# One inference step of a hybrid mLSTM/conv decoder layer: decode rows by VectorE's block transposes and DMA, and state updates as four 32-row tiles

## Chip, cores and metric

One core of one Trainium2 chip runs the whole layer. The metric is the device time in microseconds (us) of one launch.

## The reference, cut to what matters

A layer is: half a SwiGLU feed-forward (FFN), a mixer, half a second FFN, with a root-mean-square norm before and after each. The input has a prompt of 256 tokens and 8 decode sequences of 4 tokens each (32 decode tokens), 288 tokens in all, with 2048 features. The mixer projects to q, k, v, an output gate (4 heads of 256), to two halves of a gated causal convolution of width 31 over 1024 channels, and to an input and a forget gate for each head. For each head and sequence it computes

```
C_t = f_t C_{t-1} + i_t k_t v_t^T          n_t = f_t n_{t-1} + i_t k_t
h_t = o_t * (q_t C_t) / max(|n_t . q_t|, exp(-m_t))
```

in a chunkwise form with the running maximum m as stabiliser. A decode sequence starts from its own state C (256x256 for each head and sequence), n and m; its new state is `C_new = g_state * C + sum over its 4 tokens of g_key * k v^T`. All is float32. The outputs are the tokens, the new C, n, m and the convolution's history.

## The kernel before, in words

Features lie on the 128 partitions, tokens in the free dimension. All large products are weight tiles of 128x128 (stationary) against 288 tokens (moving). To keep float32's precision with one-pass matmuls, weights and activations are split into a high and a low part, and each product is three matmuls: high by high, high by low, low by high (`multiply`, L477 to L484).

**The stream of pieces.** The weights are one stream of 656 pieces of 128x1024 (8 tiles, 24 matmuls). SyncE's queue loads piece g into slot g mod 4 of `raw` as soon as the low part of piece g-4 is made (L428 to L435). ScalarE makes the high part `whi` (`split_hi`, L891, three pieces ahead of the matmuls), VectorE or GpSimd the low part `wlo` (L1312, L1859). TensorE works through the pieces. The first FFN has 264 pieces, the mixer's projections begin at piece 266 (`HEAD_P`) and have 94 more (`MIX`), then come the output projection and the second FFN.

**The mixer.** Its projection tiles are ordered by hand. `KEYS_AT` (8, 30, 54, 78) is the piece at which head h's k, v and q tiles begin; `CONV_AT` and `GATE_O_AT` are the same for convolution and output gate. Each engine's program runs over the same piece number p, and for each head h does in step k = p - KEYS_AT[h] what the hand-written order says (`head_part` in L1123, L1652, L2008; `gate_part` in L1193, L1757, L2032). TensorE puts a head's small matmuls between the tiles of the stream (`between`, L777): at (k, j) they stand after tile j of piece k.

For head h the steps that the change touches are:

- k = 8: ScalarE copies the 32 decode columns of k and v four times side by side (`kv4`, L1155); VectorE transposes the prompt's values in blocks of 32x32 (L1668). k = 10: ScalarE's queue stores those to DRAM (`store_squares`, L1115), and k = 12 loads them back token by token (`vtok`, L1178).
- (9, 5): TensorE transposes `kv4` in four matmuls (`to_token_major`, L670). k = 10: ScalarE copies the result three times (`vs`, `v4`, `k4`, L1166 to L1168). k = 11: VectorE makes the low parts in place, in other quarters of the partitions (L1681, L1685). So `k4` and `v4` hold the decode rows as 4 groups of 32 partitions, high and low parts such that one matmul over 128 partitions sums the three products.
- k = 12, 13: ScalarE masks `v4` for each of the 8 sequences (`vm`, L1187).
- k = 12: VectorE scales the decode queries (`qw`) and multiplies by the old normaliser `n0` (L1694 to L1703); k = 13 the masked scores; k = 14 the decode part of the convolution, with the taps read from SBUF (`conv_decode`, L1617); k = 15 the denominators.
- TensorE: scores (13, ..), `query_memory` (`QUERY_AT`: 32 matmul instructions on four tiles of 32 columns side by side, L707), `attend` (`ATTEND_AT`, L732 to L736, into banks 5 and 6).
- `update_memory` (L739): for each of the 8 sequences two matmuls of 128 rows and 256 columns into bank 4 or 7, at k = 16 to 18 plus `LATE` (2, 0, 0, 3); VectorE adds each to C (L1741).
- The gate: VectorE multiplies the heads in banks 5 and 6 (L1765), ScalarE makes the high part `mh` (L1206), VectorE the low part `ml` (L1769, counts `mix_ready`). For head 3 these are at GATE_O_AT[3] + 6 and + 7, pieces 96 and 97.
- k = 19: ScalarE's queue stores the weighted keys (L1115 again).

Of the kernel before, what the change touches and what calls it, by code (L numbers as in the profile page):

```python
# [23 lines left out]
F32 = mybir.dt.float32  # L24
# [82 lines left out]
Q_GROUP = 4  # L107

# [67 lines left out]
def hybrid_layer_kernel(nc, stream, x_in, vecs, gate_w, gate_vec, c_in, n_in, conv_in,  # L176
                        y_out, cp_out, np_out, cs_out, ns_out, m_out, conv_out):
    with ExitStack() as ctx:
# [38 lines left out]
        turned_v = nc.dram_tensor("turned_v", [SEQ // NS, NS, DC, H, P // NS, NS], F32, kind="Internal").ap()  # L217
        turned_k = nc.dram_tensor("turned_k", [SEQ // NS, NS, DC, H, P // NS, NS], F32, kind="Internal").ap()
# [10 lines left out]
        mh = place("mh", [P, D_MLSTM // P, TOK], F32R)  # L229
        ml = place("ml", [P, D_MLSTM // P, TOK], F32R)  # L230
# [11 lines left out]
        vtok = place("vtok", [P, 2, DH])  # L242
        k4 = place("k4", [P, DH], F32R)
        v4 = place("v4", [P, DH], F32R)
# [12 lines left out]
        vm = place("vm", [P, NB, DH], F32R)  # L257
        late_kv = place("late_kv", [P, 2, 2, H * DH], F32, xl_at)
# [7 lines left out]
        mask4 = place("mask4", [P, 4, NB], F32, prod_at)  # L266
# [8 lines left out]
        mask = place("mask", [P, NB])  # L275
# [9 lines left out]
        def squares(h):  # L285
            flat = prod[:, :, :, :].rearrange("p t b k -> p (t b k)") if h < H - 1 else bc[:, 0, :]
            return flat[:, 0:DC * SEQ].rearrange("p (c s) -> p c s", c=DC)

        key_squares = qkvo[:, 2, :, :].rearrange("p c t -> p (c t)")[:, 0:DC * SEQ].rearrange("p (c s) -> p c s", c=DC)

        ysum = rpost
        own = bass.AP(ident, 0, [[P, P], [Q_GROUP * NT, NB // Q_GROUP], [NS + NT, Q_GROUP], [1, NT]])
        qct = sq[:, :, :].rearrange("p a t -> p (a t)")[:, 0:DH]
        kv4 = cpr[:, :, :].rearrange("p c e -> p (c e)").rearrange("p (a c m) -> p a c m", a=2, c=DC)
        psum = ctx.enter_context(nc.psum_tensor("bank", [P, 8, 512], F32))
        bank = [psum[:, i, :] for i in range(8)]

# [36 lines left out]
        tr_done, dec_hi, dec_lo, vm_ready, tr_evicted = (sem("tr_done"), sem("dec_hi"), sem("dec_lo"),  # L334
                                                         sem("vm_ready"), sem("tr_evicted"))
        kv4_ready = sem("kv4_ready")
# [17 lines left out]
        nn_ready = sem("nn_ready")  # L354
        cap_ready, cap_added = sem("cap_ready"), sem("cap_added")
        turn_ready, sums_ready = sem("turn_ready"), sem("sums_ready")
# [26 lines left out]
        def four(ap):  # L383

            return ap.unsqueeze(2).broadcast_to([P, DC, P // NS, NS])
# [19 lines left out]
        def _(sp):  # L405
# [22 lines left out]
            with sp.Fori(2, PIECES // SLOTS) as m:  # L428
                for s in range(SLOTS):

                    sp.wait_ge(lo_ready[s], m * 1)
                    sp.dma_start(raw[:, s, :], stream[m * SLOTS + s]).then_inc(landed[s], 16)
# [32 lines left out]
        def _(pe):  # L465
# [204 lines left out]
            def to_token_major(h):  # L670

                pe.wait_ge(kv4_ready, h + 1)
                pe.wait_ge(col_ready, 1)
# [6 lines left out]
                mm.then_inc(tr_done, 1)  # L680

            def scores(h):

                pe.wait_ge(tile_evicted, tile_of(h, "q1") + 1)
                pe.wait_ge(dec_lo, h + 1)
# [5 lines left out]
                for c in range(DC):  # L691
                    mm = pe.matmul(bank[7][:, SEQ + P:SEQ + P + NS], kv4[:, 0, c, :], q[:, c, SEQ:TOK],
                                   start=(c == 0), stop=(c == DC - 1))
                mm.then_inc(sc_done, 1)

            def query_memory(h):
# [7 lines left out]
                for r in range(NB // Q_GROUP):  # L704
                    for c in range(DC):
                        for j in range(Q_GROUP):
                            mm = pe.matmul(bank[4][NS * j:NS * (j + 1), 0:DH], qw[:, c, r, :],  # L707
                                           C[:, r * Q_GROUP + j, c, :], start=(r + c == 0),
# [13 lines left out]
            def attend(h):  # L722

                pe.wait_ge(v_landed, 32 * (h + 1))
                pe.wait_ge(sums_ready, h + 1)
                pe.wait_ge(qc_evicted, h + 1)
                if h:
                    pe.wait_ge(mix_ready, 2 * h)
                for e in range(DC):
                    out = bank[5 + e]  # L730
                    cols = slice(e * P, (e + 1) * P)
                    pe.matmul(out[:, 0:SEQ], vtok[:, 0, cols], st[:, 0:SEQ], start=True, stop=False,  # L732
                              skip_group_check=True)
                    pe.matmul(out[:, P:SEQ], vtok[:, 1, cols], st[:, SEQ:SEQ + P], start=False, stop=True,
# [4 lines left out]
            def update_memory(h, b):  # L739

                if b < 2:
                    pe.wait_ge(den_ready if b == 0 else qc_evicted, h + 1)
                else:
                    pe.wait_ge(cu_evicted, NB * h + b - 1)
                pe.wait_ge(vm_ready, NB * h + b + 1)
                out = bank[4 if b % 2 else 7]
                for c in range(DC):
                    mm = pe.matmul(out[:, c * DH:(c + 1) * DH], k4[:, c * P:(c + 1) * P], vm[:, b, :],  # L748
                                   start=True, stop=True)
                mm.then_inc(cu_done, 1)  # L750

            def prompt_memory(h):
# [7 lines left out]
                for c in range(DC):  # L760
                    for t in range(2):
                        v = late_kv[:, 0, t, :].rearrange("p (c h e) -> p c h e", c=DC, h=H)[:, :, h, :]
# [14 lines left out]
            def between(p, j):  # L777


                for h in range(H):  # L780
# [3 lines left out]
                    if (k, j) == (9, 5):  # L784
                        to_token_major(h)
# [9 lines left out]
                    if b is not None:  # L795
                        update_memory(h, b)
# [1375 lines left out]
```

## Time and profile before

| what | value |
|---|---|
| median of 3 runs | 2153.84 us (2153.32 to 2154.47) |
| the profiled execution | 2154.55 us, of which the span of the instructions is 2152.8 |
| TensorE matmuls busy | 2145.0 us, 100% of the span, 16248 instructions |
| VectorE / ScalarE / GpSimd busy | 982.1 (46%) / 891.3 (41%) / 959.4 (45%) |
| DMA | 377.69 MB, 175 GB/s, about half of the 16 engines' time |
| granted TensorE clock | full, in all 40 slices |

A matmul's duration in the profile is from its start to the end of its results and overlaps with the next ones; what it costs in a stream is the distance from its start to the next start. The sum of idle times in front of a group is shown behind it with what released the engine.

### The profile page before, as it was taken

What the parts mean: (1) busy time and instruction counts of PE and PEld (TensorE: products, weight loads), DVE (VectorE), ACT (ScalarE), POOL (GpSimd) and SP (SyncE); (2) the same over time, 40 slices, a digit from 0 to 9 for tenths busy, and PEclk for the clock granted to TensorE, in tenths of its full rate; (3) what the DMA queues carried; (4) which work ended last, traced back from release to release, by engine and by line L of the source; (5) the groups of instructions that cost most, each with busy time, mean ns of one, the idle gap of its engine ahead of it and who ended that gap; (6) DMA issues with size and microseconds to landing.
All of it is one profiled execution on the core that took longest, in us unless ns stands there. A gap on an engine that the chain in (4) does not pass through costs nothing.

```text
span 2152.8 us, 41799 instructions
## 1 busy us (share of the span) xinstructions
PE 2145.0 (100%) x16248; PEld 2134.2 (99%) x16248; DVE 982.1 (46%) x1422; ACT 891.3 (41%) x1151; POOL 959.4 (45%) x563
## 2 busy tenths in 40 slices
PE   9999999999999999999999999999999999999998
PEld 9999999999999999999999999999999999999998
DVE  6533432223434324987769738543432223333323
ACT  6434333334343335644345446434333333333443
POOL 1444443434444445476756332444443334444444
PEclk9999999999999999999999999999999999999999
DMA  7454455545554554566766554555455545454653
GB/s 250 165 169 162 164 168 169 163 161 172 164 167 158 174 165 149 204 195 237 242 198 223 200 164 145 170 165 167 157 172 169 166 157 171 161 173 157 210 165 130
DMA packets 121860, 377.69 MB, mean 175 GB/s; under 512 B 28552, under 2 KB 33804, under 8 KB 120496
## 3 DMA queue, kind: packets, MB, share of 16 engines
q1 hardware_dynamic: 97632, 349.00, 49.2%
q10 hardware_dynamic: 24016, 27.42, 4.0%
q8 instruction: 62, 1.02, 0.2%
q14 instruction: 22, 0.18, 0.0%
q0 software_dynamic: 128, 0.07, 0.0%
HBM read 361.26 MB, written 15.18 MB: 175 GB/s over the span
## 4 chain that ended last, share of the span: by engine, by line
PE 99%; DVE 0%; DMA 0%; SPq 0%; ACT 0%; issue 0%
PE bank L484 30%; PE bank L482 30%; PE bank L483 30%; PE bank L537 1%; PE bank L544 1%; PE bank L548 1%; PE bank L826 1%; PE bank L828 1%; PE bank L827 1%; PE bank L748 0%; PE bank L707 0%; DMA raw<-stream 0%; PE bank L689 0%; DVE x_res L1416 0%; DVE bank L1415 0%; PE bank L732 0%
## 5 line engine op out<-in xcount | busy, mean ns | idle before, releaser
L1864 POOL TENSOR_TENSOR wlo<-raw,whi 128x1024 fp32r<-128x1024 f32 x331 | 794.5, 2402 | 851.8 <-ACT whi L898 771.9
L482 PE MATMUL bank<-xh,whi 128*128 128x288 f32 x3344 | 992.2, 297 | 0.0
L483 PE MATMUL bank<-xl,whi 128*128 128x288 f32 x3344 | 988.3, 296 | 0.0
L484 PE MATMUL bank<-xh,wlo 128*128 128x288 f32 x3344 | 986.4, 295 | 0.0
L898 ACT ACTIVATE whi<-raw 128x1024 fp32r<-128x1024 f32 x652 | 687.3, 1056 | 597.6 <-PE bank L484 555.1
L1317 DVE TENSOR_TENSOR wlo<-raw,whi 128x1024 fp32r<-128x1024 f32 x323 | 469.4, 1455 | 769.5 <-ACT whi L898 768.2
L482 PEld LDWEIGHTS bank<-xh,whi 128*128 128x128 f32 x3344 | 630.2, 188 | 2.4 <-issue 2.2
L484 PEld LDWEIGHTS bank<-xh,wlo 128*128 128x128 f32 x3344 | 629.7, 188 | 0.0
L483 PEld LDWEIGHTS bank<-xl,whi 128*128 128x128 f32 x3344 | 628.7, 188 | 0.2
L484 PE MATMUL bank<-hh,wlo 128*128 128x288 f32 x1408 | 417.4, 296 | 0.0
L482 PE MATMUL bank<-hh,whi 128*128 128x288 f32 x1408 | 416.1, 296 | 0.0
L483 PE MATMUL bank<-hl,whi 128*128 128x288 f32 x1408 | 410.5, 292 | 0.0
L483 PEld LDWEIGHTS bank<-hl,whi 128*128 128x128 f32 x1408 | 268.4, 191 | 0.0
L482 PEld LDWEIGHTS bank<-hh,whi 128*128 128x128 f32 x1408 | 264.5, 188 | 0.0
L484 PEld LDWEIGHTS bank<-hh,wlo 128*128 128x128 f32 x1408 | 263.8, 187 | 0.0
L1887 POOL TENSOR_TENSOR scr<-scr 128x288 f32<-128x288 f32 x88 | 74.6, 847 | 208.0 <-ACT scr L987 208.0
L991 ACT ACTIVATE hh<-scr 128x288 f32 (+1 forms) x88 | 39.1, 444 | 275.6 <-DVE scr L1455 275.6
L987 ACT ACTIVATE scr<-scr 128x288 f32<-128x288 f32 x88 | 39.2, 446 | 220.7 <-DVE scr L1434 220.7
L1434 DVE TENSOR_TENSOR scr<-bank,rstd 128x288 f32<-128x288 f32 x176 | 80.2, 456 | 76.5 <-PE bank L484 72.3
L1613 DVE SCALAR_TENSOR_TENSOR bank<-upad,vec,bank 128x256 f32<-128x256 f32 x232 | 92.8, 482 | 0.1
L1877 POOL TENSOR_TENSOR ssq<-ssq,sq 128x288 f32<-128x288 f32 x45 | 36.4, 809 | 79.8 <-ACT sq L1050 54.7
L1457 DVE TENSOR_TENSOR hl<-scr,hh 128x288 f32 (+1 forms) x88 | 40.3, 458 | 64.0 <-ACT hh L991 64.0
(262 smaller groups left out, 1264.1 us busy)
## 6 DMA issues: line engine op xcount, KB each, us to landing
raw<-stream SPq DMA_DIRECT2D x654, 512.0 KB, 3.6
C<-c_in ACTq DMA_DIRECT2D x4, 2048.0 KB, 8.8
cs_out<-C ACTq DMA_DIRECT2D x4, 2048.0 KB, 8.9
y_out<-x_res SPq DMA_DIRECT2D x7, 288.0 KB, 2.8
bc<-row_copy ACTq DMA_DIRECT2D x4, 448.0 KB, 8.9
conv_out<-upad ACTq DMA_DIRECT2D x4, 302.0 KB, 5.5
upad<-conv_in ACTq DMA_DIRECT2D x4, 272.0 KB, 3.8
vtok<-turned_v ACTq DMA_DIRECT2D x8, 128.0 KB, 3.1
```

Of the source, the lines that this page charges most:

```text
L482: pe.matmul(out, wh, mov_hi[:, k, :], start=first, stop=False)
L483: pe.matmul(out, wh, mov_lo[:, k, :], start=False, stop=False)
L484: return pe.matmul(out, wl, mov_hi[:, k, :], start=False, stop=last)
L898: act.activation(whi[:, g % SLOTS, :], raw[:, g % SLOTS, :], ACT.Copy).then_inc(hi_ready, 1)
L987: act.activation(scr[:, 2, :], scr[:, f % 2, :], ACT.Sigmoid).then_inc(sig_ready, 1)
L991: act.activation(hh[:, k, :], scr[:, 4, :], ACT.Copy).then_inc(h_hi, 1)
L1317: dve.tensor_tensor(wlo[:, g % SLOTS, :], raw[:, g % SLOTS, :], whi[:, g % SLOTS, :].bitcast(F32), ALU.subtract).then_inc(lo_ready[g % SLO ...
L1434: ins = dve.tensor_tensor(out, src, rstd[:, :], ALU.mult)
L1457: dve.tensor_tensor(hl[:, k, :], scr[:, 4, :], hh[:, k, :].bitcast(F32), ALU.subtract)\
L1613: ins = dve.scalar_tensor_tensor(out=out, in0=up_prompt(j, SEQ, k), scalar=w, in1=acc, op0=ALU.mult, op1=ALU.add)
L1864: pool.tensor_tensor(wlo[:, g % SLOTS, :], raw[:, g % SLOTS, :], whi[:, g % SLOTS, :].bitcast(F32), ALU.subtract).then_inc(lo_ready[g % SL ...
L1887: pool.tensor_tensor(scr[:, 5 + f % 2, :], scr[:, f % 2, :], scr[:, 2, :], ALU.mult)\
```

## The change

- The block transposes of k = 8 now also take the 32 decode columns of v and k (4 more of 128x32). ScalarE's queue stores them (`store_decode`, 4 DMAs, at k = 9 + `ROWS_LATER`, which is (1, 0, 0, 1); `SP_AHEAD` is 7), and the prompt's blocks one step later. SyncE's queue loads both back, between pieces: `decode_rows` (4 DMAs of 32 partitions) and `value_rows` (1 DMA), each behind a wait for the stores and for the last reader.
- ScalarE scales the loaded rows at k = 13 + `ROWS_LATER` (5 activations), GpSimd sums two parts to the operands `both4` one step later. TensorE's transposes, the three copies and VectorE's low parts go.
- The 128 partitions are now 4 groups of 32, one for a pair of sequences; each group holds the three products' parts. `update_memory` runs twice for a head, for 4 sequences each time: 2 x 4 matmuls on tiles of 32 rows, into banks 7, 4, 5, 6. It stands at (17, 1) and (18, 3) plus `LATE`. Two masks instead of eight.
- Banks 5 and 6 are now needed by the updates: for heads 0 to 2 ScalarE first copies the attended heads to SBUF (`heads`), and the gate works there; for head 3 the first update waits until the gate's `ml` is made (`mix_ready`).
- The old normaliser and the decode taps are copied to unused columns of bank 6 by ScalarE at k = 11, and VectorE reads them there. Head 0's reciprocal is one step later. A few small set-up instructions are added.

```diff
+DEC_LOAD = {KEYS_AT[h] + 11 + ROWS_LATER[h] + SP_AHEAD: h for h in range(H)}
+VTOK_LOAD = {KEYS_AT[h] + 12 + ROWS_LATER[h] + SP_AHEAD: h for h in range(H)}
...
+            def decode_rows(h):
+                sp.wait_ge(dec_stored, 64 * (h + 1))
+                if h:
+                    sp.wait_ge(dec_sums, h)
+                for q in range(Q_GROUP):
+                    rows_of = turned_d[h][UNIT * q:UNIT * (q + 1), :, :].rearrange("u i x -> u (i x)")
+                    sp.dma_start(dec[NS * q:NS * (q + 1), :, :, :, :].rearrange("p i n c a -> p (i n c a)"),
+                                 rows_of.unsqueeze(0).broadcast_to([COPIES, UNIT, 2 * DH])).then_inc(dec_landed, 16)
...
-            def to_token_major(h):
...
-                for j, src in enumerate((2, 1)):
-                    for c in range(DC):
-                        mm = pe.transpose(bank[7][:, (2 * j + c) * P:(2 * j + c + 1) * P],
-                                          kv4[:, src - 1, c, :], ident[:, :])
...
-            def update_memory(h, b):
+            def update_memory(h, n):
+                if n:
+                    pe.wait_ge(cu_evicted, NB * h + Q_GROUP)
                 else:
-                    pe.wait_ge(cu_evicted, NB * h + b - 1)
-                pe.wait_ge(vm_ready, NB * h + b + 1)
-                out = bank[4 if b % 2 else 7]
+                    pe.wait_ge(den_ready, h + 1)
+                    pe.wait_ge(qc_evicted, h + 1)
+                    pe.wait_ge(vm_ready, PAR * (h + 1))
+                    if h < H - 1:
+                        pe.wait_ge(heads_kept, DC * (h + 1))
+                    else:
+                        pe.wait_ge(mix_ready, DC * H)
                 for c in range(DC):
-                    mm = pe.matmul(out[:, c * DH:(c + 1) * DH], k4[:, c * P:(c + 1) * P], vm[:, b, :],
-                                   start=True, stop=True)
-                mm.then_inc(cu_done, 1)
+                    for g in range(Q_GROUP):
+                        rows_of = slice(NS * g, NS * (g + 1))
+                        mm = pe.matmul(bank[UPDATE_BANK[g]][:, c * DH:(c + 1) * DH], both4[rows_of, 1, c * P:(c + 1) * P],
+                                       vm[rows_of, n, :], start=True, stop=True, tile_position=(NS * g, 0))
+                        if c == DC - 1:
+                            mm.then_inc(cu_done, 1)
...
-            updates = {(16, 1): 0, (16, 4): 1, (16, 7): 2, (17, 2): 3, (17, 5): 4, (18, 0): 5, (18, 3): 6, (18, 6): 7}
+            updates = {(17, 1): 0, (18, 3): 1}
```

## Rows read from the trace of the kernel before

**Rows 1.** The page: busy time (share of span), and the chain that ended last.

```profile
PE 2145.0 (100%) x16248; PEld 2134.2 (99%) x16248; DVE 982.1 (46%) x1422; ACT 891.3 (41%) x1151; POOL 959.4 (45%) x563
...
PE 99%; DVE 0%; DMA 0%; SPq 0%; ACT 0%; issue 0%
```

**Rows 2.** Windows, 890 to 1200 us: busy (instructions) by engine, clock, DMA.

```profile
890.00:1200.00 310.00, 310.00 (x2403) 304.23 (x2402) 249.04 (x516) 146.96 (x204) 196.87 (x118) 1.00 0.66 218
```

**Rows 3.** Timeline of PE, head 0's first update (start, duration, line, count).

```profile
949.85 0.29 PE L484 MATMUL bank<-xh,wlo 128*128 128x288 f32 x1
949.98 0.40 PE L748 MATMUL bank<-vm,k 128*128 128x256 f32 x2
950.22 0.29 PE L482 MATMUL bank<-xh,whi 128*128 128x288 f32 x1
950.35 0.30 PE L483 MATMUL bank<-xl,whi 128*128 128x288 f32 x1
```

**Rows 4.** The groups by line: all updates of the four heads.

```profile
L748 PE MATMUL bank<-vm,k 128*128 128x256 f32 x64 | 12.7, 279 | 0.0
```

**Rows 5.** Timeline of PE, head 0's transposes.

```profile
916.48 0.60 PE L678 MATMUL bank<-ident,cpr 128*128 128x128 f32 x4
916.83 0.38 PE L482 MATMUL bank<-xh,whi 128*128 128x288 f32 x1
917.05 0.30 PE L483 MATMUL bank<-xl,whi 128*128 128x288 f32 x1
```

**Rows 6.** Timeline of PE, head 0's query on four column tiles, and its attend.

```profile
940.87 0.29 PE L484 MATMUL bank<-xh,wlo 128*128 128x288 f32 x1
941.09 1.93 PE L707 MATMUL bank<-C,qw 128*32 128x256 f32 x32
942.96 0.40 PE L482 MATMUL bank<-xh,whi 128*128 128x288 f32 x1
943.19 0.29 PE L483 MATMUL bank<-xl,whi 128*128 128x288 f32 x1
...
946.65 0.59 PE L732 MATMUL bank<-st,vtok 128*128 128x256 f32 x2
947.08 0.38 PE L734 MATMUL bank<-st,vtok 128*128 128x128 f32 x2
```

**Rows 7.** Timeline of the weight loads (PEld) just after that query.

```profile
942.96 0.19 PEld L482 LDWEIGHTS bank<-xh,whi 128*128 128x128 f32 x1 [0.41 <-issue]
943.06 0.19 PEld L483 LDWEIGHTS bank<-xl,whi 128*128 128x128 f32 x1
```

**Rows 8.** The groups by line: ScalarE's masks, VectorE's additions to C.

```profile
L1187 ACT ACTIVATE vm<-v,mask 128x256 fp32r<-128x256 f32 x32 | 13.6, 496 | 4.9 <-issue 4.9
...
L1741 DVE SCALAR_TENSOR_TENSOR C<-C,bc,bank 128x512 f32<-128x512 f32 x32 | 23.5, 742 | 13.0 <-PE bank L748 13.0
```

**Rows 9.** The page's DMA issues: KB each, median us to landing.

```profile
raw<-stream SPq DMA_DIRECT2D x654, 512.0 KB, 3.6
...
vtok<-turned_v ACTq DMA_DIRECT2D x8, 128.0 KB, 3.1
```

**Rows 10.** Timelines around head 3's first update: PE, ACT (twice), DVE.

```profile
1201.92 0.40 PE L748 MATMUL bank<-vm,k 128*128 128x256 f32 x2
...
1201.41 3.79 ACTq L1115 DMA_DIRECT2D turned_k<-qkvo  x4
1205.24 0.71 ACT L1206 ACTIVATE mh<-bank 128x288 fp32r<-128x288 f32 x2 [2.80 <-issue]
...
1205.89 0.82 DVE L1769 TENSOR_TENSOR ml<-bank,mh 128x288 fp32r<-128x288 f32 x2
```

**Rows 11.** Timeline of ACT: the same four stores of head 0.

```profile
953.13 2.66 ACTq L1115 DMA_DIRECT2D turned_k<-qkvo  x4
```

**Rows 12.** Timelines of DVE and PE at mixer piece 31.

```profile
963.79 1.74 DVE L1317 TENSOR_TENSOR wlo<-raw,whi 128x1024 fp32r<-128x1024 f32 x1
...
967.00 0.30 PE L482 MATMUL bank<-xh,whi 128*128 128x288 f32 x1
```

More of the change, by code:

```diff
@@ L229, in hybrid_layer_kernel @@
         mh = place("mh", [P, D_MLSTM // P, TOK], F32R)
+        heads = place("heads", [P, D_MLSTM // P, TOK], F32, arena[0])
         ml = place("ml", [P, D_MLSTM // P, TOK], F32R)
@@ L274, in hybrid_layer_kernel @@
         ntmp = place("ntmp", [P, DC, NB])
-        mask = place("mask", [P, NB])
+        mask = place("mask", [P, PAR])
+        side = place("side", [P, 2, 2])
+        colv = place("colv", [P, 2, H])
         qwn = place("qwn", [P, DC, NS])
@@ L793, in between @@
                         attend(h)
-                    b = updates.get((k - LATE[h], j))
-                    if b is not None:
-                        update_memory(h, b)
+                    n = updates.get((k - LATE[h], j))
+                    if n is not None:
+                        update_memory(h, n)
                 if (p, j) == (MIX_FROM, 3):
@@ L1153, in head_part @@
                     act.wait_ge(tile_evicted, tile_of(h, "v1") + 1)
-                    for n in range(2):
-                        last = act.activation(kv4[:, n, :, :].rearrange("p c (j t) -> p c j t", j=P // NS),
-                                              four(qkvo[:, 1 + n, :, SEQ:TOK]), ACT.Copy)
-                    last.then_inc(kv4_ready, 1)
-                if k == 10:
-                    act.wait_ge(tr_done, h + 1)
+                    if h:
+                        act.wait_ge(sc_done, h)
@@ new lines, in head_part @@
+                    for c in range(DC):
+                        last = act.activation(in_copies(keys4[:, c, :]), copied(qkvo[:, 1, c, SEQ:TOK]), ACT.Copy)
+                    last.then_inc(keys4_ready, 1)
+                if k == 9 + ROWS_LATER[h]:
+                    act.wait_ge(v_turned, h + 1)
+                    store_decode(h)
+                if k == 10 + ROWS_LATER[h]:
+                    store_squares(turned_v, h, squares(h), v_stored)
+                if k == 13 + ROWS_LATER[h]:
+                    act.wait_ge(dec_landed, 64 * (h + 1))
+                    act.wait_ge(colv_ready, 1)
+                    act.wait_ge(turn_ready, 2)
@@ L1169, in head_part @@
[L1169 to L1178 removed]
+                    act.activation(natural(vs[:, :]), in_order(dec, 0), ACT.Copy, scale=turn[:, 1:2])
@@ L1761, in gate_part @@
                     for e in (0, 1) if late else (o // 2 - 2,):
-                        dve.wait_ge(num_done, 3 * h + 3)
                         dve.wait_ge(ro_ready, 2 * h + e + 1)
-                        head = bank[5 + e][:, 0:TOK]
-                        dve.tensor_tensor(head, head, qkvo[:, 3, e, :], ALU.mult).then_inc(hm_ready, 1)
+                        if late:
+                            dve.wait_ge(num_done, 3 * H)
+                            head = bank[5 + e][:, 0:TOK]
+                        else:
+                            dve.wait_ge(heads_kept, DC * h + e + 1)
+                            head = heads[:, DC * h + e, :]
+                        dve.tensor_tensor(gated_head(h, e), head, qkvo[:, 3, e, :], ALU.mult).then_inc(hm_ready, 1)
                 if o in ((7,) if late else (6, 8)):
```

310 lines of the change are left out of this document (196 added, 114 removed).

## The prediction

> **What bounds the kernel.** I read the page first: TensorE is busy for the whole span and 99% of the chain that ended last is its own work [rows 1]. Then the windows of the mixer, where alone the change works: in 310 us TensorE never pauses, the clock granted is full (the 2.4 GHz level), VectorE is busy 249 us, GpSimd 197, ScalarE 147 [rows 2]. So the time is the sum of the distances between matmul starts, 2145.0 us / 16248 = 0.132 us each [rows 1], and only two things move it: matmuls that go or get cheaper, and new waits of TensorE. Work of other engines counts where it makes TensorE wait. The timeline of TensorE prices the small matmuls, the one of the other engines around each new wait shows who comes last.
>
> **Transposes removed.** Four start at 916.48 and the second matmul of the stream behind them at 917.05: 0.57 us where one ordinary distance of 0.13 would stand, so 0.44 a head and 1.75 us for four [rows 5].
>
> **Updates, old price.** From the L484 before an update to the L483 behind it are 0.50 us; without it these are two distances, 0.26. A sequence costs 0.236 us, the 32 of them (64 matmuls) 7.6 us, and the four that one new round replaces 0.94 [rows 3, 4].
>
> **Updates, new price.** No row shows tiles of 32 rows. The nearest is the query on four tiles of 32 columns: 32 instructions from L484 at 940.87 to L483 at 943.19, 2.32 us, less two distances 2.06. A full-width instruction with the same 256 moving columns and two such passes costs 0.215 (946.65 to 947.08 for two), so four abreast would be 32 x 0.215 / 4 = 1.72 [rows 6]. Tiles do run side by side, and entering and leaving them costs 0.34: 0.09 before the first, 0.15 inside, 0.10 behind the last. A new round is two sets of four matmuls; a one-pass matmul of 256 columns costs 0.12 [rows 3], so the sets take 0.24. To that comes the 0.34, and the first load is of 128 columns, not 32: two such loads stand 0.10 apart [rows 7], so some 0.08 more. Together 0.66, against 0.94: 0.28 saved a round, 2.3 us for eight. The bounds: no price for entering (0.24 a round, 5.6 us saved), or loads of 128 columns one after the other, 8 x 0.10 + 0.12 + 0.34 = 1.26 a round, 2.6 us lost. I take the middle, since the query shows loads and matmuls of four tiles side by side and it is the nearest row.
>
> The Trainium skill's page "TensorEngine Tiling (Array Packing)", section "Key Properties", says that changing the tiling mode drains the engine, whichever mode it is; by that the toll would be due for row tiles too, 16 more changes of mode, and the cheap bound could not come true. The query's 0.34 agrees with it for column tiles; no row shows it for row tiles.
>
> **A new wait, head 3.** Banks 5 and 6 hold the attended heads, and the first update of head 3 writes into them, so it waits for the gate's last low part (`mix_ready` of 8). In the old order the first update stood at 1201.92; the new place, one piece later with no update between, is 24 x 0.132 = 3.17 us on, at 1205.09. ScalarE's queue at that step first issues the four stores of the keys, 3.79 us from 1201.41, and only then makes `mh` (1205.24 to 1205.95); VectorE's second `ml` takes 0.41 more, so 1206.4 [rows 10]. ScalarE's step begins on a TensorE event, so this distance moves with the matmuls. TensorE waits 1.3 us. Head 0's same four stores took 2.66 [rows 11]; then the wait would be 0.2. I take 1.3, the row of the place itself, and keep 0.2 as the other end. Behind it on TensorE's queue is the whole stream: all of the wait lands in the time.
>
> **Other edits, costed at nothing, and what covers them.**
> - ScalarE: gone are 2 copies, 3 evictions and 6 of 8 masks a head (a mask 0.50) [rows 8]; new are 2 copies, 5 scalings, 2 copies of heads, 2 small ones. Equal within a microsecond. Its queue issues 4 stores more and 2 loads less, about 0.66 each [rows 11], 1.3 us a head. It is idle half of the mixer [rows 2] and splits three pieces ahead (9.5 us).
> - ScalarE's new wait for the decode rows, at step 13: behind it are the splits, and behind these TensorE. SyncE's queue issues the four loads in step 11 (some 2.6 us of issue), a load of rows lands in 3.1 [rows 9]: 5.7 us against two steps of 3.2. Late by little, it eats into the 9.5.
> - SyncE's queue: 5 more DMAs a head between pieces, about 3.3 us of issue. A piece is loaded four steps (12.7 us) before ScalarE needs it and lands in 3.6 [rows 9]: 9 us to spare. The value rows have three and a half steps, 11 us, until `attend`.
> - GpSimd: one addition a head, 512 columns, with a third of its time free [rows 2]. Its set-up runs while it waits.
> - VectorE loses three low parts and gains four small transposes. Additions to C come four in a row, 4 x 0.742 = 3.0 us [rows 8]; the next round waits for them and stands 30 matmuls, 4.0 us, behind the first. 1 us to spare; next late would be this.
> - The tightest low part in the mixer is piece 31's: VectorE ends it at 965.53, TensorE wants it at 967.00 [rows 12]. Four additions instead of a last single one end about 0.6 us later in step 28, so the room shrinks from 1.5 to some 0.8 us. If it were gone, the excess would be paid once.
> - Reading old normaliser and taps from PSUM saves VectorE time that nobody waits for.
>
> **The sum.** -1.75 - 2.3 + 1.3 = -2.7 us. Against the profiled execution (2154.55, span 2152.8 and 1.8 around it) that is 2151.8; its time stands 0.7 above the median of the three runs, so of the median 2151.1. A measurement of this kernel can tell about 0.2% (4.3 us) from no change; this is less.
>
> **Rivals.**
> A, *tiles without a toll* (chance 0.22): entering and leaving 32-row tiles is nearly free, a round costs 0.24 to 0.35. For it: the toll is measured on column tiles only. Against: it is there in every query. 5.6 saved instead of 2.3: 2153.84 - 1.75 - 5.6 + 1.3 = 2147.8.
> The Trainium skill's page "TensorE: Matmul & The Clock Gate", section "Measured speedup vs the span model", gives 3.07x for four row tiles of 512 columns; by that a round would be 0.94 / 3.07 = 0.31 and the whole an estimated -5.5 us. No row here shows row tiles.
>
> B, *loads in turn* (0.13), the one that ends slower: each of a round's eight matmuls needs its own load of 128 columns, and if those cannot overlap between row groups a round costs 1.26. 2153.84 - 1.75 + 2.6 + 1.3 = 2156.0. It turns from gain to loss where a round costs over 0.94 + (1.75 - 1.3) / 8 = 1.0 us. The same price would show if the tiles did not run side by side at all, the case that the change doesn't do what it says. For it: 128-column loads follow each other at 0.10 [rows 7], nearly the matmul's own 0.12. Against: four loads for four column tiles overlapped in the query.
> The Trainium skill's page "TensorE: Matmul & The Clock Gate", section "LDWEIGHTS (loading the stationary operand)", says that a load takes as long for 32 rows as for 128, since the columns count; this speaks against the change and would, with loads in turn, give B's time.
>
> C, *rows late* (0.10): store, wait, load and scaling are now a chain over three queues. If the rows land more than three steps late, TensorE waits for high parts, a step of 3.2 us or so for each head: 2151.1 + 4 x 3.2 = 2164. Against: 9 us of room on each link [rows 9].
>
> The forecast has 0.55, with a range of its own of 2149.9 (wait of 0.2) to 2151.5.
>
> **Numbers.** 2151.1 us. The range 2147.6 to 2156.2 takes in A and B with their bounds and leaves out C and a tail of A. Faster by over 0.2%: A and a little of the forecast's edge, 0.27. Slower by over 0.2%: C, 0.10. Within: 0.63.
>
> **What the changed profile would show.** The matmul count falls by 16, transposes are gone. In TensorE's timeline a group of 8 updates occupies about 0.66 us between L484 and L483 beyond the two distances (0.24 to 0.35 under A, 1.2 under B). Head 3's first update has a wait in front of it whose releaser is VectorE's `ml`, 1.3 us or 0.2; the other seven rounds none. If a wait of TensorE stands anywhere else in the mixer, at pieces 31, 46 or 70 above all, C or the piece-31 room was misjudged. If the FFNs outside 890 to 1220 us changed their length, the sum as a whole is wrong.

## The result, and the profile after

| | before | changed |
|---|---|---|
| median of the timed runs | 2154.03 us (20 runs, 2153.32 to 2156.4) | 2159.02 us (20 runs, 2154.91 to 2162.49) |
| profiled execution, its span | 2154.55, 2152.8 us | 2156.58, 2154.8 us |

The ratio is 1.0023, with a 95% interval of 1.0017 to 1.0030: slower by 5.0 us. The forecast was 2151.1, the range ended at 2156.2, and slower by over 0.2% had 0.10. Two things need explaining: the profiled execution is 2.0 us longer than before where 2.7 less was forecast, and it is itself one of the three shortest of the twenty; the other seventeen are 1.5 to 5.9 us longer still. The times of the kernel before lie within 1.3 us of each other except for one, those of the changed kernel within 7.6. The mean granted clock of each execution is a first hint: 0.999 to 1.000 in the three shortest, 0.998 or 0.997 in sixteen of the other seventeen.

The page of the changed kernel, its busy line and its chain, beside [rows 1]:

```profile
PE 2142.2 (99%) x16232; PEld 2128.6 (99%) x16232; DVE 995.7 (46%) x1436; ACT 887.4 (41%) x1148; POOL 969.5 (45%) x573
...
PE 92%; DVE 5%; POOL 1%; issue 1%; ACT 1%; DMA 0%; ACTq 0%; SPq 0%; DVEq 0%; POOLq 0%
```

TensorE has 16 matmuls fewer and is busy for 2.8 us less, in a span 2.0 us longer. The chain of before was TensorE's own; now VectorE holds 5% of it. VectorE is busy for 13.6 us more. The same window as [rows 2] places most of that in the mixer (249.0 to 260.7 us of VectorE, 310.00 to 304.73 of TensorE); taken from 890 to 1230 us, it is 13.5 (270.0 to 283.5):

```profile
890.00:1200.00 310.00, 304.73 (x2367) 296.22 (x2366) 260.73 (x526) 140.62 (x198) 204.10 (x122) 1.00 0.67 220
```

The waits of TensorE in the mixer (engine, tile and line that waited, the releaser, total, times, longest); the kernel before has none there:

```profile
PE bank L844 <- POOL rpost L2124: 2.1, 1, 2.1
PE bank L800 <- DVE sq L1824: 1.3, 1, 1.3
PE bank L757 <- DVE qkvo L1618: 1.2, 1, 1.2
PE bank L848 <- DVE lnb L1894: 0.5, 1, 0.5
PE bank L558 <- POOL wlo L1972: 0.2, 1, 0.2
```

L757 is head 0's scores, L800 head 1's attend, L844 and L848 the two sums of the layer norm while head 3 runs. As distances between matmul starts these waits cost 6.5 us (with the slower first matmul behind a wait, and one more distance that is 0.25 too long). None stands at head 3's first update, where the wait was forecast.

The first update round, in the timeline of TensorE, beside [rows 3] and [rows 5]:

```profile
953.69 0.29 PE L560 MATMUL bank<-xh,wlo 128*128 128x288 f32 x1
953.91 0.51 PE L822 MATMUL bank<-vm,both 32*128 32x256 f32 x8
954.35 0.40 PE L558 MATMUL bank<-xh,whi 128*128 128x288 f32 x1
954.59 0.30 PE L559 MATMUL bank<-xl,whi 128*128 128x288 f32 x1
```

From L560 to L559 are 0.90 us; less two distances of 0.132, a round costs 0.64, against 0.94 for the four sequences that it replaces. Inside, four matmuls start within 12 ns, the second four 0.22 later. TensorE saved 8 x 0.30 + 1.75 = 4.15 us, the 4.05 of the forecast, and lost 6.5: between the same two pieces of the stream before and behind the mixer the changed kernel is 2.3 us longer, and 0.3 shorter ahead of it.

Who was late? The groups of VectorE's instructions in the mixer follow (busy, mean ns of one). In the kernel before the gate takes 457 ns and `ml` 448 in the mean, eight of each:

```profile
L1872 DVE TENSOR_TENSOR qkvo<-heads,qkvo 128x288 f32<-128x288 f32 x6 | 9.6, 1599 | 1.4 <-POOL qkvo L2166 1.4
L1876 DVE TENSOR_TENSOR ml<-qkvo,mh 128x288 fp32r<-128x288 f32 x6 | 8.8, 1474 | 0.0
L1762 DVE TENSOR_SCALAR colv<-col,side 128x4 f32<-128x4 f32 x2 | 3.9, 2012 | 0.0
L1876 DVE TENSOR_TENSOR ml<-bank,mh 128x288 fp32r<-128x288 f32 x2 | 0.8, 453 | 0.9 <-ACT mh L1299 0.9
L1872 DVE TENSOR_TENSOR bank<-bank,qkvo 128x288 f32<-128x288 f32 x2 | 0.8, 437 | 0.0
```

One instruction, two prices: 1.5 us in the mean where both inputs lie in SBUF (heads 0 to 2), 0.44 where one lies in PSUM (head 3). And a product of 128 x 4 takes 2.0. The timelines of VectorE and GpSimd show what these have in common (start, duration; the second block is GpSimd):

```profile
1134.26 2.63 DVE L1872 TENSOR_TENSOR qkvo<-heads,qkvo 128x288 f32<-128x288 f32 x1 [0.68 <-POOL qkvo L2166]
1136.82 6.35 DVE L1709 SCALAR_TENSOR_TENSOR bank<-upad,vec,bank 128x256 f32<-128x256 f32 x16
...
1143.46 0.44 DVE L1872 TENSOR_TENSOR qkvo<-heads,qkvo 128x288 f32<-128x288 f32 x1
```

```profile
1134.19 2.39 POOL L1972 TENSOR_TENSOR wlo<-raw,whi 128x1024 fp32r<-128x1024 f32 x1
1137.10 2.40 POOL L1972 TENSOR_TENSOR wlo<-raw,whi 128x1024 fp32r<-128x1024 f32 x1 [0.51 <-ACT whi L971]
...
1143.44 5.57 POOL L1972 TENSOR_TENSOR wlo<-raw,whi 128x1024 fp32r<-128x1024 f32 x2 [0.77 <-ACT whi L971]
```

GpSimd starts a low part at 1134.19, VectorE's gate starts at 1134.26 and ends at 1136.89, 0.3 behind the end of GpSimd's instruction. At 1143.4 the two start within 20 ns of each other; this time the gate takes 0.44, and it is GpSimd's low part that is long (two in 5.57 instead of 4.8, which is the gate and the `ml` behind it, 0.81). The sixteen conv taps between (L1709, one input in PSUM) run over GpSimd's instructions at their usual 0.4 us each. So the reading: **a VectorE instruction that reads two tensors of SBUF, or scales one from SBUF to SBUF, stands still until GpSimd's running instruction ends, and the other way round; with an input in PSUM it does not.**

No run moves GpSimd's work, so its part rests on the traces, but they are plain. VectorE's own low parts (128x1024, two SBUF inputs) split in two in the changed kernel's profile: 135 start while GpSimd is idle and take 1.23 us at most; 188 start inside a GpSimd instruction, take 1.61 in the mean, and none of them ends before that instruction does. GpSimd's low parts take 2.40 us; the eight that start inside a VectorE `tensor_tensor` with two SBUF inputs take 2.76 in the mean.

The Trainium skill states this on the page "SBUF — State Buffer", section "Who interferes with whom": a VectorE instruction with two SBUF inputs and a GpSimd instruction that reads SBUF exclude each other, a VectorE instruction in a mode with two ports (a `tensor_scalar` can enter one) and a GpSimd instruction do too, and whoever issues second is blocked until the other is done. The rows agree, with the 2.63 and the 0.44 above.

**How this becomes waits.** Head 0: the two `colv` hold VectorE from 908.22 to 912.16, everything behind them comes that much later, `q` is evicted at 930.1 (928.0 in the kernel before), and the scores wait. Head 3: the gate at 1134.26 takes 2.63 instead of 0.47 and `ml` at 1150.83 takes 1.68; the conv's sums leave GpSimd's hands 2.4 us later (its L2124 starts at 1163.35, its old L2005 at 1160.91), and TensorE's ln_mean waits 2.1. VectorE had been idle for 61 us of the window before, but from the gate (1134 to 1135) to the last conv sum (1161 before, 1163 now) it works without a pause, in both kernels, so there a delay goes through to the end undiminished.

### The profile page after: what moved, and what is told of

Read it like the earlier page. It is cut to its first block, busy times and chain, and to the rows that moved or that the text cites. A ratio compares the mean times of both kernels' runs of the same rounds, so it can differ in the third digit from the quotient of the medians.

```text
span 2154.8 us, 41461 instructions
## 1 busy us (share of the span) xinstructions
PE 2142.2 (99%) x16232; PEld 2128.6 (99%) x16232; DVE 995.7 (46%) x1436; ACT 887.4 (41%) x1148; POOL 969.5 (45%) x573
## 4 chain that ended last, share of the span: by engine, by line
PE 92%; DVE 5%; POOL 1%; issue 1%; ACT 1%; DMA 0%; ACTq 0%; SPq 0%; DVEq 0%; POOLq 0%
PE bank L560 28%; PE bank L558 28%; PE bank L559 28%; DVE bank L1709 3%; PE bank L613 1%; PE bank L624 1%; PE bank L620 1%; PE bank L899 1%; PE bank L901 1%; PE bank L900 1%; POOL wlo L1972 1%; PE bank L631 0%; DVE ml L1876 0%; PE bank L775 0%; ACT whi L971 0%
## 5 line engine op out<-in xcount | busy, mean ns | idle before, releaser
L559 PE MATMUL bank<-xl,whi 128*128 128x288 f32 x3344 | 988.3, 296 | 0.0
L560 PE MATMUL bank<-xh,wlo 128*128 128x288 f32 x3344 | 986.4, 295 | 0.0
L560 PEld LDWEIGHTS bank<-xh,wlo 128*128 128x128 f32 x3344 | 629.8, 188 | 0.0
L559 PEld LDWEIGHTS bank<-xl,whi 128*128 128x128 f32 x3344 | 628.7, 188 | 0.2
L560 PE MATMUL bank<-hh,wlo 128*128 128x288 f32 x1408 | 417.4, 296 | 0.0
L559 PE MATMUL bank<-hl,whi 128*128 128x288 f32 x1408 | 410.5, 292 | 0.0
L559 PEld LDWEIGHTS bank<-hl,whi 128*128 128x128 f32 x1408 | 268.4, 191 | 0.0
L560 PEld LDWEIGHTS bank<-hh,wlo 128*128 128x128 f32 x1408 | 263.8, 187 | 0.0
L1709 DVE SCALAR_TENSOR_TENSOR bank<-upad,vec,bank 128x256 f32<-128x256 f32 x232 | 92.7, 478 | 0.0
```

Of the source, the lines that this page charges most:

```text
L559: pe.matmul(out, wh, mov_lo[:, k, :], start=False, stop=False)
L560: return pe.matmul(out, wl, mov_hi[:, k, :], start=False, stop=last)
L1709: ins = dve.scalar_tensor_tensor(out=out, in0=up_prompt(j, SEQ, k), scalar=w, in1=acc, op0=ALU.mult, op1=ALU.add)
```

## The experiments

**Theory S** (the reading above) had as rivals: the new rows of the decode values come late over three queues (C), tiles of 32 rows bring the clock down (T), a gate with any operand in PSUM is free (D). Ten kernels ran, eleven executions each (six of e3), beside the kernel before, whose median stayed between 2153.95 and 2154.15. The code is cut to the lines that matter.

### e3: one part of the change, in the kernel before

```
# ScalarE, step 16 + LATE, heads 0 to 2
+ act.activation(heads[:, DC * h + e, :], bank[5 + e][:, 0:TOK], ACT.Copy)
# VectorE's gate and ml, ScalarE's mh
- dve.tensor_tensor(head, head, qkvo[:, 3, e, :], ALU.mult)       # head = bank[5 + e]
+ dve.tensor_tensor(qkvo[:, 3, e, :], heads[:, DC * h + e, :], qkvo[:, 3, e, :], ALU.mult)
```

> The kernel before with one part of the change alone: ScalarE copies the attended heads 0 to 2 to SBUF, the gate and its low part ml read and write SBUF. Old update order, old transposes, no rows on SyncE, no tiles of 32 rows, no colv. Theory S: gates 1.6 and ml 1.5 us in the mean instead of 0.45; ln_mean of head 3 waits about 2.2 us and perhaps head 1's attend and ln_squares too: slower than before by 2.2 to 5 us, with a scatter of the times as the changed kernel has it. Rival (rows late, longer queues of ScalarE and SyncE, or the tiles bring the clock down): as before, 2154.0 +- 0.5.

Measured: 2160.36 us (2157.24 to 2166.38), ratio 1.0033 [1.0021, 1.0045]. ScalarE's next sigmoid also waits for `ml` there, since it overwrites the same tile. None of the change's savings, no tiles, no new rows, and the kernel is as slow and scattered as the changed one. Its groups and its one wait:

```profile
L1777 DVE TENSOR_TENSOR qkvo<-heads,qkvo 128x288 f32<-128x288 f32 x6 | 9.5, 1585 | 1.1 <-POOL qkvo L2050 1.1
L1781 DVE TENSOR_TENSOR ml<-qkvo,mh 128x288 fp32r<-128x288 f32 x6 | 6.9, 1151 | 0.0
```

```profile
PE bank L682 <- ACT cpr L1159: 2.7, 2, 2.1
```

The durations came as expected. The waits did not stand at ln_mean, as S had it, but at two of the transposes that the change has removed: head 1's (0.8 us as a distance) and head 3's, just before ln_mean (2.3). They wait for ScalarE's copy of the decode columns, and that copy had itself waited 5.7 us for VectorE's eviction. C and T are not needed for a loss of this size, though this run does not exclude them beside it.

### e1: where the gate's result goes

```
 def gated_head(h, e):
-    return qkvo[:, 3, e, :] if h < H - 1 else bank[5 + e][:, 0:TOK]
+    return bank[5 + e][:, 0:TOK]
...                                # attend of heads 1 to 3, whose output goes to the same banks
+    pe.wait_ge(mix_ready, 2 * h)
```

> The changed kernel, but VectorE writes the gated head into PSUM (banks 5 and 6, free again by then) instead of into qkvo, so that the gate reads two SBUF tiles and writes PSUM, and the low part ml reads one PSUM and one SBUF tile. Theory S (a VectorE instruction whose two tensor inputs both lie in SBUF, or a tensor_scalar from SBUF to SBUF, stands still until GpSimd's running instruction ends; one with a PSUM input does not): all six ml take 0.45 us instead of 1.47 in the mean, the six gates keep their 1.6, because where the result goes does not matter. Head 1's attend then waits less than 0.5 us instead of 1.5; ln_mean of head 3 still waits about 2.3, since the gate at 1134 us is the one that makes it late. Profiled execution some 1.5 us below the changed kernel's 2156.6. Rival D (any PSUM operand, output too, frees the instruction): the gates also take 0.45, all waits of head 1 and head 3 go (5 us less). Rival C (rows late on SyncE and ScalarE): nothing moves.

Measured: 2157.17 us (2154.91 to 2159.51), ratio 1.0014 [1.0006, 1.0023]; profiled span 2155.4.

```profile
L1873 DVE TENSOR_TENSOR bank<-heads,qkvo 128x288 f32<-128x288 f32 x6 | 9.5, 1576 | 1.5 <-POOL qkvo L2167 1.5
L1877 DVE TENSOR_TENSOR ml<-bank,mh 128x288 fp32r<-128x288 f32 x8 | 3.5, 443 | 0.0
```

The clearest test of the two: an output in PSUM frees nothing (1576 ns), an input in PSUM does (443). D is out. Head 1's attend no longer waits, and ln_mean waits 0.9 instead of 2.1, where 2.3 was expected. The time fell by 1.9 in the median, but the profiled execution did not (2157.17): a wait that had not been there stood at head 3's first update, 1.8 us.

### e2: the two tiny products

```
- dve.tensor_scalar(colv[:, n, :], col[:, 5, :], side[:, n, 1:2], None, ALU.mult)
+ dve.tensor_scalar(colv[:, n, :], bank[7][:, 5 * H:6 * H], side[:, n, 1:2], None, ALU.mult)
...                                # head 0's scores, which go to bank 7
+ pe.wait_ge(colv_ready, 1)
```

> The changed kernel, but the two 128 x 4 products colv read bank 7 (PSUM) instead of col (SBUF); nothing else. Theory S: they take about 0.1 us each instead of 3.9 together, q of head 0 is evicted some 3.8 us earlier, and the wait of head 0's scores (1.4 us) is gone, the others stay: the profiled execution is 1.5 us below 2156.6 and the timed runs fall by 1.5 us or, if this wait is also one that brings the clock down, by more. Rival (tiny instructions are slow by themselves, whatever they read): colv stays near 2 us each and nothing moves.

Measured: 2157.05 us (2153.58 to 2161.55), ratio 1.0018 [1.0009, 1.0026].

```profile
L1763 DVE TENSOR_SCALAR colv<-bank,side 128x4 f32<-128x4 f32 x2 | 0.4, 218 | 0.0
```

218 ns instead of 2012: not tininess but the place of the input made them slow. The wait of the scores went, that of head 1's attend too (each of the two delays alone is covered there), and the wait at head 3's update came, as in the kernel above.

### e4: both, with a PSUM input for every one

```
# ScalarE, output steps 3 and 5 of heads 0 to 2
+ act.activation(bank[5 + e][:, 0:TOK], heads[:, DC * h + e, :], ACT.Copy)
# VectorE's gate reads and writes bank[5 + e] for every head; colv as above
```

> The changed kernel with every one of these VectorE instructions given a PSUM input: ScalarE copies the kept head back into banks 5 and 6 once the state additions have left them (6 copies of 0.45 us in its idle half), the gate multiplies there as in the kernel before, ml and mh read PSUM, colv reads bank 7. Theory S: gates, ml 0.45 us each, colv 0.2 together; all five waits of TensorE go; what is left is the saving of 1.75 + 2.4 = 4.15 us: 2149.9 us against 2154.0, with the scatter of the kernel before (below 1 us) and clock 1.000. Rival C (rows late, queues): the attend wait of head 1 stays, 1.5 us. Rival T (32-row tiles bring the clock down): times scatter up to 2156 although no wait is left.

Measured: 2152.44 us (2150.20 to 2154.06), ratio 0.9990 [0.9981, 0.9999]: 6.6 us below the changed kernel, 1.5 below the one before, and 2.5 above the 2149.9 that was expected. Gates take 454 ns, `ml` 446. C is out as a cause: its wait, of head 1's attend, is gone though every row still travels as in the changed kernel. The waits that are left:

```profile
PE bank L825 <- DVE ml L1883: 1.8, 1, 1.8
PE bank L851 <- DVE lnb L1901: 0.4, 1, 0.4
```

The first is the wait that the prediction had named, by its releaser, `ml`. It costs 1.9 us as a distance, and this is why 2149.9 was missed. Its cause was not the one named. The timeline of VectorE:

```profile
1199.03 3.42 DVE L1418 TENSOR_TENSOR wlo<-raw,whi 128x1024 fp32r<-128x1024 f32 x1
1202.37 0.81 DVE L1883 TENSOR_TENSOR ml<-bank,mh 128x288 fp32r<-128x288 f32 x2
```

and of GpSimd:

```profile
1198.74 2.62 POOL L1979 TENSOR_TENSOR wlo<-raw,whi 128x1024 fp32r<-128x1024 f32 x1 [7.01 <-ACT whi L974]
```

ScalarE had `mh` ready at 1200.45 (its four stores took 2.07 us, not the 3.79 of [rows 10]); but VectorE's low part, two SBUF inputs, had started 0.29 us behind GpSimd's and stood until that ended. The same low part took 3.42 us, behind GpSimd's, in the profiles of e1 and e2, and the same wait followed. In the kernel before VectorE's came first and took 1.21 us; GpSimd's took 2.94. The times of this kernel lie in two clusters, five of 2150.2 to 2150.9 and six of 2152.4 to 2154.1. That the lower cluster had no such wait is the likely reading, since the next kernel, without the wait, lies near it; it has no profile of its own, so this is not shown.

### e5 and e6: head 3's rounds later

```
  updates = {(17, 1): 0, (18, 3): 1}
+ late_updates = {(17, 6): 0, (18, 7): 1}      # head 3
```

> The kernel of e4_all_psum_inputs, with head 3's two rounds moved down the stream by 15 and 12 matmuls (2.0 and 1.6 us); the other heads as they were. There the first round waited 1.9 us for ml and the granted clock fell behind such a wait in two of the profiles. Theory: the wait is gone, 2.0 us less: profiled execution 2148.7 to 2149.0, no stretch at 1.2 GHz, and the timed runs, which stood at 2150.2 to 2154.1 in two clusters (with and without such a stretch, 3.4 us long and worth 1.7 us, or two of them), fall to 2148.5 to 2149.5. Rival (the clock falls because 32-row tiles keep the array less busy): the wait goes, but the times still lie in two clusters some 3 us apart.

Measured: 2150.89 us (2150.48 to 2151.84), ratio 0.9986 [0.9977, 0.9995]; profiled execution 2150.57, span 2148.8. Its busy and chain lines:

```profile
PE 2140.7 (100%) x16232; PEld 2127.9 (99%) x16232; DVE 982.0 (46%) x1436; ACT 888.8 (41%) x1154; POOL 966.7 (45%) x573
...
PE 99%; DVE 1%; issue 0%; POOL 0%; ACT 0%; POOLq 0%
```

The span fell by the 1.9 us of the wait, and the scatter shrank from 3.9 to 1.4 us. The collision of the low parts is still there (3.42 us); TensorE now comes later than its outcome. The expected figure for the time was 1.7 us too low: it took the span for the execution. T is out: 64 matmuls on tiles of 32 rows, and the granted clock is full through the whole mixer. VectorE's busy time is that of the kernel before (982.0 to 982.1). The median is 8.1 us below the changed kernel's and 3.2 below the one before; e7 and e8, variants of this kernel, measure the same.

```
- late_updates = {(17, 6): 0, (18, 7): 1}
+ late_updates = {(17, 3): 0, (18, 5): 1}
```

> As e5_head3_update_later, but head 3's rounds moved by 6 matmuls only (0.8 us): a wait of about 1.2 us is left instead of 2.0 or none. Theory (a wait brings the clock down, the longer the oftener): times between: 2149.9 without a fall of the clock, at 2151.6 and above with one, fewer of these than with the wait of 2.0. Rival (a wait costs its own length and nothing more): all at 2149.9 +- 0.4.

Measured: 2152.57 us (2151.25 to 2153.05), ratio 0.9992 [0.9983, 1.0001]. The wait was 1.1 us as expected, and the second one, of 0.5 in the kernel above, for VectorE's first output (`y`), grew to 1.1; together that is the 1.7 between the medians. Both expected figures were too low, the 2149.9 for the same reason as in e5 and because the second wait was not counted. The times form one cluster and the profile shows no fall of the clock, so the rival is nearer, at this length of wait. The mean clocks (0.999 to 1.000) can't tell: they are the same in e5, and one fall changes them by 0.001.

### e9 and e10: each stall put back alone in e5

```
- dve.tensor_scalar(colv[:, n, :], bank[7][:, 5 * H:6 * H], side[:, n, 1:2], None, ALU.mult)
+ dve.tensor_scalar(colv[:, n, :], col[:, 5, :], side[:, n, 1:2], None, ALU.mult)
```

> The kernel of e5_head3_update_later (2150.9 us, no long wait) with one stall put back: colv is computed from SBUF again, as in the changed kernel. Theory S: the two products take 4.0 us together instead of 0.2, q of head 0 comes that much later, head 0's scores wait 1.4 us plus 0.1 for the slower first matmul: 2152.4, in some runs 1.7 more where the clock falls behind the wait. Rival (four microseconds of VectorE in a stretch where it waits for others anyway are free): 2150.9.

Measured: 2151.80 us (2151.43 to 2152.71), ratio 0.9989 [0.9980, 0.9998]. The products take 2042 ns again and the scores wait 1.3 us; the span is 1.7 us longer than without, the median 0.9, where 1.5 was expected.

```
- act.activation(bank[5 + e][:, 0:TOK], heads[:, DC * h + e, :], ACT.Copy)
- dve.tensor_tensor(bank[5 + e][:, 0:TOK], bank[5 + e][:, 0:TOK], qkvo[:, 3, e, :], ALU.mult)
+ dve.tensor_tensor(qkvo[:, 3, e, :], heads[:, DC * h + e, :], qkvo[:, 3, e, :], ALU.mult)
```

> The kernel of e5_head3_update_later with the other stall put back: gates and ml of heads 0 to 2 in SBUF, as in the changed kernel; colv stays in PSUM. Theory S: six gates 1.6 and six ml 1.1 to 1.5 us; head 3's sums reach ln_mean 2.3 us late, small waits at mixer piece 90 and ln_squares: 2150.9 + 2.3 + 0.4 = 2153.6 without a fall of the clock, 1.7 more for each stretch at 1.2 GHz: median 2154 to 2157, scatter of several microseconds as in the changed kernel. Together with e9 the two stalls make up the 2159.0 of the changed kernel. Rival (the loss of the changed kernel has another half, in rows and queues): this kernel stays at 2151 to 2152.

Measured: 2154.31 us (2153.36 to 2158.57), ratio 1.0006 [0.9997, 1.0015], in two clusters: six runs of 2153.4 to 2154.3 and five of 2157.1 to 2158.6. The profile is of the upper one:

```profile
PE bank L845 <- POOL rpost L2126: 5.3, 1, 5.3
PE bank L558 <- DVE y L1935: 0.5, 1, 0.5
```

ln_mean waits 5.3 us here, where 2.3 was expected. VectorE and GpSimd at the place where the gate took 0.44 in the changed kernel's profile:

```profile
1140.08 2.59 DVE L1874 TENSOR_TENSOR qkvo<-heads,qkvo 128x288 f32<-128x288 f32 x1
1142.59 0.45 DVE L1878 TENSOR_TENSOR ml<-qkvo,mh 128x288 fp32r<-128x288 f32 x1
```

```profile
1139.96 2.40 POOL L1974 TENSOR_TENSOR wlo<-raw,whi 128x1024 fp32r<-128x1024 f32 x1 [0.77 <-ACT whi L973]
```

GpSimd was 0.12 us ahead, and the gate took 2.59. In the changed kernel the two started within 20 ns and it took 0.44. Two engines that are not tied to each other meet at this point, and which comes first decides over 2.1 us; at 1149.6 the same happened to an `ml` (2.60, against 1.68 there). This is the likely source of the scatter; the lower cluster has no profile.

The windows of the same profile show what a long wait does besides (length, busy times, then the granted clock behind POOL's column):

```profile
1162.44:1169.27 6.83, 3.46 (x12) 3.17 (x13) 5.40 (x13) 4.36 (x8) 6.07 (x6) 0.50 0.25 82
1169.27:1176.10 6.83, 6.83 (x54) 6.83 (x53) 6.76 (x7) 4.88 (x7) 4.40 (x3) 1.00 0.74 207
```

While TensorE waited (it had started nothing since 1160.24), its clock fell to 1.2 GHz, and for 3.4 us behind the wait its matmuls stood 0.24 apart instead of 0.13, which costs some 1.6 us more. Such a stretch followed the waits of 1.9 us in the profiles of e1 and e2 at head 3's update (in e1 from 1207.85 to 1211.26, with 17 matmuls, and 31 in the next 3.4 us) and the one of 2.3 in that of e3, and none of the waits of 1.1 to 1.5 in any profile. The waits for ln_mean in the profiles of the changed kernel and of e2 (2.1) and that of 1.9 in e4, the same wait as in e1 and e2, had none either: at this length it goes both ways. One stretch of 3.4 us at half the clock lowers the mean clock of an execution by 0.0008. Sixteen of the changed kernel's twenty executions, its median among them, have 0.998 or 0.997, so more than one such stretch each is likely; none of the sixteen has a profile.

### e7 and e8: two questions on the side, both in e5

```
- taps = taps_bank[:, j * TAPS:(j + 1) * TAPS] ...      old = n0_bank ...
+ taps = bass.AP(vec, V_TAP + n * TAPS, ...)            old = n0[:, h, :, :]
```

> As e5_head3_update_later, but the old normaliser and the decode taps are read from SBUF again, as in the kernel before (ScalarE still makes its copies, nobody reads them). Theory S: prod (two SBUF inputs) of heads 0 to 2 takes 1.2 to 3.6 us again instead of 1.18, qwn up to 2 us instead of 0.18; VectorE is later by 2 to 5 us a head at steps 12 and 14. My prediction costed this part at nothing, since VectorE's time there is nobody's: then the time stays within 0.5 us of e5's. Rival (this part carries weight): head 1's or head 0's attend waits for qct again, 1 to 2 us more each.

Measured: 2151.04 us (2150.56 to 2152.16), ratio 0.9986 [0.9977, 0.9995], 0.15 from the kernel with them in PSUM. `prod` took 1416 ns in the mean instead of 1183 where it reads PSUM; nobody waited for it.

```
- for c in range(DC):              + for g in range(Q_GROUP):
-     for g in range(Q_GROUP):     +     for c in range(DC):
```

> As e5_head3_update_later, but a round's eight matmuls go tile by tile (both column halves of row group 0, then of row group 1, and so on) instead of all four groups for one half and then for the other. It asks why a round costs 0.64 us beyond the distances of the stream and not the 0.24 of two sets of matmuls. Theory (each tile's own load has to wait for that tile's last matmul, other tiles' loads run beside it): in this order the second matmul of each tile waits for its load before the next tile can start, since TensorE issues in order: four times 0.21 instead of two, a round costs 1.0 to 1.1 us, the kernel 8 x 0.4 = 3.2 us more than e5. Rival (the order does not matter, the toll is the change of tile size alone): the same 0.64.

Measured: 2150.80 us (2150.52 to 2151.32), ratio 0.9985 [0.9976, 0.9994]. A round:

```profile
952.05 0.29 PE L561 MATMUL bank<-xh,wlo 128*128 128x288 f32 x1
952.27 0.52 PE L825 MATMUL bank<-vm,both 32*128 32x256 f32 x8
952.72 0.40 PE L559 MATMUL bank<-xh,whi 128*128 128x288 f32 x1
952.96 0.30 PE L560 MATMUL bank<-xl,whi 128*128 128x288 f32 x1
```

0.91 us from L561 to L560 instead of 0.90: the theory was wrong, a tile's second matmul doesn't hold up the next tile's. In either order four matmuls start within 10 to 20 ns, and the next four from 0.22 us after the first. Only the second matmul of each tile raises a semaphore, and in this kernel's trace too these are the four that start last, 0.22 us behind their tile's first. So the next tile's first matmul starts 7 ns after the one before it, past a second one that stands ahead of it in the program. What the 0.22 consists of stays open. The rival's 0.64 holds, that it is the change of tile size was not tested by itself. The Trainium skill's page "TensorEngine Tiling (Array Packing)", section "Key Properties", says that a change of tiling mode drains the engine; the 0.09 us before the first matmul and 0.11 behind the last agree with it, now for tiles of 32 rows too. But 0.09 also stands behind head 0's transposes, on the full array (916.83 to 917.05 in [rows 5]), so the part behind need not come from the tiles.

## Why the prediction was wrong

- **Transposes, -1.75**: right; the group is gone and TensorE has 16 matmuls fewer.
- **Update rounds, -2.3**: right. 0.64 us a round against 0.66, so -2.4. Rivals A (0.24 to 0.35) and B (1.26) are both excluded: all eight rounds lie within 4 ns of each other.
- **New wait, head 3, +1.3**: in the changed kernel absent, because TensorE came there later by its waits at the layer norm, and VectorE's `ml` (done at 1206.97) was no longer last for it (1207.46). Once those were gone it stood there at 1.8 to 1.9, behind `ml` as forecast. The place and the releaser were right, the cause and the size were not: not the four stores of ScalarE (2.07 us in e4) but a low part of VectorE behind GpSimd's.
- **"Other edits, costed at nothing"**: this is the step that failed, in its line on VectorE, "VectorE loses three low parts and gains four small transposes". It counted instructions gone and come, and put the rest at nothing; in its place stand three waits of TensorE, 1.4, 1.5 and 2.3 us as distances. The change also moved operands: six gates and six `ml` now read two tiles of SBUF, and `colv` is new and goes from SBUF to SBUF. Twelve instructions became 1.0 to 1.1 us longer each in the mean and two cost 3.9. The line on PSUM and the normaliser was right (e7), and so was ScalarE's and SyncE's part: no wait of TensorE traces back to the rows once VectorE is in time.
- **What could have been seen**: that VectorE's 249 busy of 310 us [rows 2] are no reserve where a chain through it ends at TensorE, and a row of the trace before that was not read, VectorE in head 1:

```profile
1034.06 2.35 DVE L1755 TENSOR_TENSOR nns<-ntmp,nred 128x16 f32<-128x16 f32 x1
```

```profile
1033.99 2.39 POOL L1864 TENSOR_TENSOR wlo<-raw,whi 128x1024 fp32r<-128x1024 f32 x1 [1.50 <-ACT whi L898]
```

An addition of 16 elements that takes 2.35 us and ends with GpSimd's instruction. Twelve gates and `ml` at up to 2.4 us each would have been a rival with its own place, ln_mean.
- **Rival C, rows late**: wrong, though it alone had the time slower by over 0.2%; head 1's attend did wait, and the rows did come late there (ScalarE waited 8.0 us for them once), but at most 4.0 in e4, with the same rows and VectorE in time: the rest of the lateness was VectorE's. The prediction's sign for this case, a wait of TensorE elsewhere in the mixer, did come, but it stood for C or piece 31 there, and it was neither.

**The sum again.** e5 has both savings and no long wait: 2150.89, where the forecast without its +1.3 gives 2149.8; the two small waits that are left (0.6 us each as distances, ln_squares and `y`) make the difference. From there to the changed kernel's 2159.02 are 8.1 us. Between the two profiled executions it is 6.0, of which 5.5 lie between the same two pieces around the mixer, and these are the waits for scores, attend and ln_mean (5.1) and little else. The other 2.1 lie between each kernel's profiled execution and its median; the mean clock of 0.998 in the changed kernel's longer executions points to falls of the clock, which no profile of it caught. Put back alone, the two stalls gave 0.9 and 3.4. That is 4.3 of the 8.1: they don't add up, since the two delays together reach head 1's attend, which neither reaches alone. The wait at the old place of head 3's round (1.6 between e4 and e5) is no part of it, because the changed kernel's profile doesn't have it.

## What to carry to other kernels

An edit that leaves the count and size of VectorE's instructions alone can still make them take three times as long: look for each of its inputs where it lies, and whether GpSimd is running then. If it is, one input in PSUM is worth a copy by an idle ScalarE (six copies of 0.40 us and one changed operand bought back 6.6 us here). And when times scatter over several microseconds where they used to agree within one, look for two engines that meet at one point with nothing that orders them, and let what TensorE needs stand clear of it by more than the longer outcome.

## What the hardware showed unexpectedly

- The exclusion reaches the smallest instructions here: 128 x 4 elements took 2.0 us in the mean, 128 x 16 took 2.35.
- Neither side has a right of way: GpSimd 0.07 to 0.29 us ahead, and VectorE stood (2.63, 2.59, 3.42 us); VectorE at the same moment within 20 ns, and GpSimd's was the longer.
- Four matmuls on tiles of 32 rows with loads of 128 columns start 3 to 4 ns apart, or 7 ns in the other order of the tiles. The bound of the forecast by which the loads go one after the other (0.10 each) is not approached.
- A matmul that waits for its own tile doesn't hold back another tile's that stands behind it in the program (e8).
- A wait of 1.9 to 2.3 us can cost 1.6 us more through the clock, and does so in some executions and not in others; waits of 1.1 to 1.5 us did so in no profile here.
